# Two layers of an encoder trunk: one more pair of slabs by seven products, and single norms

## What is computed

```
h    = rmsnorm(x, gain)
proj = h @ w_in                     # 1024 -> 2304 columns in layer 0
q, k = rmsnorm per head of 64; v as it is
layer 0: heads 0-7 dilated windows with ALiBi; heads 8-15 banded GQA with a sink in the denominator
layer 1: dense GQA with rotary positions
x = x + concat(heads) @ w_out
x = x + sum over experts of weight * down(silu(gate(h2)) * up(h2))   # 32 experts, 2 of them for a token
```

## Time and profile before

| | |
|---|---|
| median of three executions | 618.3 us |
| the profiled execution, its own time | 618.75 us |
| span of its trace | 616.7 us |
| TensorE busy | 565.0 us (92%) |
| VectorE / ScalarE busy | 199.0 / 136.6 us |
| read from HBM | 231.6 MB |
| layer 0 mixer, layer 0 experts | 0 to 135 us, 135 to about 318 us |

### The profile page before, as it was taken

One profiled execution on the slowest core, in us unless ns is written; L12 is line 12 of the kernel. 1 busy time (PEld: TensorE's weight loads), 2 busy tenths in 40 slices (PEclk: granted clock), 3 DMA queues, 4 the chain that ended last, 5 costly groups with the idle time before them and its releaser, 6 DMA issues.

```text
span 616.7 us, 9572 instructions
## 1 busy us (share of the span) xinstructions
PE 565.0 (92%) x3884; PEld 373.5 (61%) x3884; DVE 199.0 (32%) x613; ACT 136.6 (22%) x353; POOL 9.9 (2%) x25
## 2 busy tenths in 40 slices
PE   8999999998999939998999999999899996997897
PEld 7887777783555333555468876779355435444454
DVE  3847555153111101111045687416212011011101
ACT  3144445341001101001031366524100110110101
POOL 1200000000000000000001000000000000000000
PEclk9999999999999969999999999999999997999899
DMA  8999786589999999999999994539999999999996
GB/s 316 424 421 420 282 361 218 204 329 409 430 430 425 442 425 424 433 435 409 421 415 421 421 421 206 207 122 354 373 427 431 428 435 424 430 426 432 413 421 271
DMA packets 24245, 233.39 MB, mean 378 GB/s; under 512 B 2688, under 2 KB 3328, under 8 KB 6656
## 3 DMA queue, kind: packets, MB, share of 16 engines
q1 hardware_dynamic: 22176, 227.14, 88.6%
q10 hardware_dynamic: 2016, 5.52, 2.5%
HBM read 231.60 MB, written 1.05 MB: 377 GB/s over the span
## 4 chain that ended last, share of the span: by engine, by line
PE 70%; DMA 20%; issue 4%; DVE 3%; ACT 3%; ACTq 0%; DVEq 0%
DMA ring<-in_moe_w 18%; PE banks L1118 13%; PE banks L851 10%; PE banks L984 8%; PE banks L1092 7%; PE banks L1188 6%; PE banks L1204 6%; PE banks L866 3%; PE banks L944 2%; PE banks L823 2%; PE banks L961 2%; PE banks L972 2%; DMA desk<-in_bias 1%; PE banks L1103 1%; PE banks L995 1%
## 5 line engine op out<-in xcount | busy, mean ns | idle before, releaser
L1118 PE MATMUL banks<-ring,desk 128*32 128x512 f32 x768 | 90.1, 608 | 5.4 <-DMA ring<-in_moe_w 5.3
L1448 ACT ACTIVATE desk<-banks 128x256 f32<-128x256 f32 x16 | 6.1, 383 | 272.7 <-PE banks L1118 272.7
L851 PE MATMUL banks<-ring,hT 128*128 128x256 f32 x288 | 65.3, 381 | 0.0
L1092 PE MATMUL banks<-desk,hT 128*128 128x128 f32 x384 | 49.5, 291 | 15.4 <-issue 15.4
L984 PE MATMUL banks<-heads,ring 128*128 128x256 f32 x256 | 61.9, 387 | 0.1
L1092 PEld LDWEIGHTS banks<-desk,hT 128*128 128x128 f32 x384 | 49.0, 208 | 16.7 <-issue 16.2
L851 PEld LDWEIGHTS banks<-ring,hT 128*128 128x128 f32 x288 | 53.7, 190 | 8.6 <-issue 1.8
L1118 PEld LDWEIGHTS banks<-ring,desk 128*32 128x32 f32 x768 | 23.7, 112 | 57.0 <-issue 51.9
L984 PEld LDWEIGHTS banks<-heads,ring 128*128 128x128 f32 x256 | 46.4, 190 | 12.6 <-issue 6.9
L1204 PE MATMUL banks<-desk 128*128 128x256 f32 x224 | 52.1, 386 | 0.0
L1204 PEld LDWEIGHTS banks<-desk 128*128 128x128 f32 x224 | 41.4, 190 | 16.8 <-issue 11.7
(11 more groups left out here) (201 smaller groups left out, 649.1 us busy)
## 6 DMA issues: line engine op xcount, KB each, us to landing
ring<-in_moe_w SPq DMA_DIRECT2D x66, 1024.0 KB, 26.7
ring<-in_moe_w SPq DMA_DIRECT2D x16, 4096.0 KB, 27.5
ring<-in_moe_w SPq DMA_DIRECT2D x17, 2048.0 KB, 12.7
ring<-in_ab_w_in SPq DMA_DIRECT2D x8, 1024.0 KB, 16.8
shared<-in_moe_w SPq DMA_DIRECT2D x8, 1024.0 KB, 7.6
shared<-in_moe_w SPq DMA_DIRECT2D x2, 4096.0 KB, 27.5
shared<-in_moe_w SPq DMA_DIRECT2D x3, 2048.0 KB, 11.3
ring<-in_c_w_in SPq DMA_DIRECT2D x5, 1024.0 KB, 20.3
```

Source lines behind the costliest of these rows:

```text
L851: ins = pe.matmul(bank2(SLAB_BANK[layer][s], NT)[:, t, :], hT[:, c, t * P:(t + 1) * P], w[:, c, :], start=(c == 0 and t == 0), stop=(c == ...
L1092: ins = pe.matmul(bank(2 + half)[:, c * P:(c + 1) * P], tokens[:, t, half * HALF + c * P:half * HALF + (c + 1) * P], onehot_of(rd, to)[:, ...
L1118: ins = pe.matmul(bank(0)[j * SLOTS:(j + 1) * SLOTS, :], gathered_of(rd, place)[:, c, j * SLOTS:(j + 1) * SLOTS], w[:, j, :], start=(c == ...
```

## The change

Slabs 5 and 6, and 7 and 8, become pairs, so that three pairs stand for two and no plain slab is left after slab 2. The differences of the weights get two buffers in turn (one more slot of the ring, SUMS_AT 15), and their four instructions are items of their own. Slab 5 (values) leaves its pair by a copy that scales. Slabs 6, 7 and 8 are normed one by one. ORDER_0 is written anew behind the first pair; layer 1 and the experts keep their code.

```diff
-PAIRED = ((3, 4), (6, 7))
-SUMS_AT = 16
+PAIRED = ((3, 4), (5, 6), (7, 8))
+SUMS_AT = 15
...
-        NORM = [[(0, 1), (3, 4), (6, 7), (8,)], ...
+        NORM = [[(0, 1), (3, 4), (6,), (7,), (8,)], ...
...
-            + each("norm", 0) + each("weights", 0) + parts(2, 0, 1, 2, 3)
+            + each("norm", 0) + sums(0, 3, 1, 2, 4) + parts(2, 0, 1, 2, 3)
             + each("turn", 0) + products(0, 1) + each("turn", 1) + products(0, 5)
-            + each("scores", 0) + products(0, 6, 7) + each("normalise", 0) + products(0, 2, 3)
-            + each("turn_prob", 0) + each("scores", 1) + products(0, 4) + parts(5, 0)
-            + each("prob_values", 0) + each("normalise", 1) + parts(5, 1) + each("norm", 1) + each("weights", 1) + parts(5, 2)
-            + each("turn_prob", 1) + parts(5, 3) + each("turn", 3) + products(1, 1) + each("turn", 4) + products(1, 5)
-            + each("scores", 2) + each("prob_values", 1) + products(1, 6, 7) + each("normalise", 2) + products(1, 2)
-            + each("turn_prob", 2) + each("scores", 3) + products(1, 3) + each("prob_values", 2)
-            + products(1, 4) + each("normalise", 3) + parts(8, 0) + each("residual", 0) + each("norm", 2)
-            + each("turn_prob", 3) + parts(8, 1, 2) + each("prob_values", 3) + parts(8, 3) + each("norm", 3)
-            + each("turn", 6) + rows((0, 0), (0, 1)) + each("turn", 7) + each("residual", 1) + rows((0, 2))
-            + each("scores", 4) + rows((0, 3), (1, 0), (1, 1)) + each("normalise", 4) + each("turn", 8) + rows((1, 2))
-            + each("turn_prob", 4) + each("residual", 2) + each("scores", 5) + rows((1, 3))
-            + each("prob_values", 4) + each("normalise", 5) + rows((2, 0), (2, 1))
-            + each("turn_prob", 5) + each("scores", 6) + rows((0, 4), (1, 4))
-            + each("prob_values", 5) + each("normalise", 6) + rows((2, 2), (2, 3))
-            + each("turn_prob", 6) + each("scores", 7) + rows((2, 4), (0, 5), (1, 5)) + each("prob_values", 6)
-            + each("normalise", 7) + rows((2, 5), (0, 6), (1, 6), (2, 6)))
+            + each("scores", 0) + products(0, 6, 7) + each("normalise", 0) + sums(1, 3, 1, 2) + products(0, 2, 3)
+            + each("turn_prob", 0) + each("scores", 1) + products(0, 4) + products(1, 1)
+            + each("prob_values", 0) + each("normalise", 1) + products(1, 5) + each("norm", 1) + products(1, 6)
+            + sums(1, 4) + each("turn_prob", 1) + products(1, 7) + sums(2, 3, 1, 2) + each("turn", 3) + products(1, 2)
+            + each("turn", 4) + each("prob_values", 1) + products(1, 3) + each("scores", 2) + products(1, 4)
+            + products(2, 1) + each("normalise", 2) + products(2, 5) + each("turn_prob", 2) + each("norm", 2)
+            + each("scores", 3) + products(2, 6) + each("prob_values", 2) + products(2, 7) + sums(2, 4)
+            + each("normalise", 3) + each("turn", 6) + products(2, 2) + each("residual", 0) + each("turn_prob", 3)
+            + products(2, 3) + each("prob_values", 3) + products(2, 4) + each("residual", 1) + each("norm", 3, 4)
+            + rows((0, 0), (0, 1), (0, 2), (0, 3), (1, 0)) + each("turn", 7) + rows((1, 1), (1, 2))
+            + each("turn", 8) + each("residual", 2) + each("scores", 4) + rows((1, 3), (2, 0), (2, 1), (2, 2))
+            + each("normalise", 4) + each("turn_prob", 4) + each("scores", 5) + rows((2, 3))
+            + each("prob_values", 4) + each("normalise", 5) + rows((0, 4), (1, 4))
+            + each("turn_prob", 5) + each("scores", 6) + rows((2, 4))
+            + each("prob_values", 5) + each("normalise", 6) + rows((0, 5), (1, 5))
+            + each("turn_prob", 6) + each("scores", 7) + rows((2, 5)) + each("prob_values", 6)
+            + each("normalise", 7) + rows((0, 6), (1, 6), (2, 6)))
...
         # product j == 5 of a pair after the first (PE)
-                    slab_taken(pe, 0, first - 1 if pair else 1)
+                    pe.wait_ge(s_tiles, 3 * pair)
...
         # ACT, product 2 and product 4 of a pair whose slab is "values"
+                        A.activation(values[0][:, 0, col:col + 4 * HD], x[:, 0, :], ACT.Copy, scale=rstd[:, 0:1])
+                            A.activation(values[0][:, 1, col:col + 4 * HD], widened, ACT.Copy, scale=rstd[:, 1:2])
...
         # ACT, residual
+                if layer == 0 and cp == 0:
+                    act.wait_ge(s_c11, len(PAIRED))
+                elif layer == 0 and cp == 1:
+                    act.wait_ge(s_tiles, 3 * len(PAIRED))
...
         # DVE, second tile of the pair's second slab: the wait inside buffer_turned now holds for "heads" and "keys"
-                if SLAB_PLAN[0][s][0] != "shared2":
+                if SLAB_PLAN[0][s][0] in ("heads", "keys"):
                     dve.wait_ge(s_hT_ps, turns_before(*NORMED[norm_slabs_before(0, s) - 1]))
```

More of the change, by code:

```diff
@@ L281, in hybrid_moe_kernel @@
         token_sum = sums_of[:, 0:UNIT].rearrange("p (i c t) -> p i c t", i=4, c=NC // 2)
-        weight_sum = sums_of[:, UNIT:UNIT + 3 * D].rearrange("p (i c n) -> p i c n", i=3, c=NC // 2)
+        weight_sums = sums_of[:, UNIT:UNIT + 6 * D].rearrange("p (r i c n) -> p r i c n", r=2, i=3, c=NC // 2)
         late_tiles = shared[:, 7168:7168 + 512].rearrange("p (t n) -> p t n", t=NT)
-        kept, widened = late_tiles[:, 0, :], late_tiles[:, 1, :]
-        fifth = shared[:, 7680:7680 + 256]
+        kept, widened = shared[:, 7680:7936], shared[:, 7936:8192]
+        fifth = shared[:, 3840:4096]
         LATER = (4, PAIRS)
@@ L556, in hybrid_moe_kernel @@
         SLAB_BANK = [[6, 7, 2, 6, 7, 6, 7, 6, 7], [2, 3, 6, 7, 6, 7]]
-        NORM = [[(0, 1), (3, 4), (6, 7), (8,)], [(0,), (2,), (3,), (4,), (5,)]]
+        NORM = [[(0, 1), (3, 4), (6,), (7,), (8,)], [(0,), (2,), (3,), (4,), (5,)]]
         def parts(slab, *which):
@@ L564, in products, with sums @@
             return [("product", pair, j) for j in which]
+        def sums(pair, *which):
+            return [("weights", pair, i) for i in which]
         def rows(*pieces):
@@ L657, in unnormed, with tile_of @@
             return buffers[:, norm_slabs_before(layer, s) % 2, :].rearrange("p (t n) -> p t n", t=NT)
+        def tile_of(s, t):
+            if SLAB_PLAN[0][s][0] == "values":
+                return widened
+            return late_tiles[:, t, :] if SLAB_PLAN[0][s][0] == "shared2" else unnormed(0, s)[:, t, :]
         def pair_banks(pair):
@@ L839, in slab @@
                     b = SLAB_BANK[layer][s]
[L840 to L843, removed]
+                    if b in SLAB_BANK[layer][:s]:
                         slab_taken(pe, layer, max(k for k in range(s) if SLAB_BANK[layer][k] == b))
@@ L860, in product @@
                 wa, wb = slab_weights(0, first), slab_weights(0, second)
+                t2, t3, t4 = [weight_sums[:, pair % 2, i, :, :] for i in range(3)]
                 low_half, high_half = slice(0, NC // 2), slice(NC // 2, NC)
@@ L871, in product @@
                     if pair:
-                        slab_taken(pe, 0, PAIRED[pair - 1][1])
+                        pe.wait_ge(s_c11, pair)
                     else:
@@ L877, in product @@
                 elif j == 5:
-                    slab_taken(pe, 0, first - 1 if pair else 1)
+                    if pair:
+                        pe.wait_ge(s_tiles, 3 * pair)
+                    else:
+                        slab_taken(pe, 0, 1)
                     pe.wait_ge(s_tsum, 1)
@@ L885, in product @@
                     pe.wait_ge(s_wsum, 4 * pair + 3)
-                    multiply(x[:, 1, :], token_sum[:, 1, :, :], weight_sum[:, 0, :, :]).then_inc(s_prod, 1)
+                    multiply(x[:, 1, :], token_sum[:, 1, :, :], t2).then_inc(s_prod, 1)
                 elif j == 7:
@@ L889, in product @@
                     pe.wait_ge(s_tsum, 3)
-                    multiply(y[:, 1, :], token_sum[:, 2, :, :], weight_sum[:, 1, :, :]).then_inc(s_prod, 1)
+                    multiply(y[:, 1, :], token_sum[:, 2, :, :], t3).then_inc(s_prod, 1)
                 elif j == 2:
@@ L900, in product @@
                     pe.wait_ge(s_wsum, 4 * pair + 4)
-                    multiply(y[:, 1, :], hT[:, high_half, rows_1], weight_sum[:, 2, :, :]).then_inc(s_used, 2)
+                    multiply(y[:, 1, :], hT[:, high_half, rows_1], t4).then_inc(s_used, 2)
             def turn(layer, s, half):
@@ L1303, in take_product @@
                     product_done(act, pair, 2)
-                    room_for(first)
-                    A.activation(unnormed(0, first)[:, 0, :], x[:, 0, :], ACT.Copy).then_inc(s_c11, 1)
+                    kind, _, col, _ = SLAB_PLAN[0][first]
+                    if kind == "values":
+                        A.activation(values[0][:, 0, col:col + 4 * HD], x[:, 0, :], ACT.Copy, scale=rstd[:, 0:1])\
+                            .then_inc(s_c11, 1)
+                        return
+                    if kind != "shared2":
+                        room_for(first)
```

(32 more changed lines are left out.)

2 lines of the change are left out of this document (removed).

## The result

The changed kernel takes 631.7 us (median of six executions, 630.84 to 634.34) against 618.41 for the kernel before (618.0 to 619.19): 2.24% slower, ratio 1.0224, 95% interval 1.0201 to 1.0248. The forecast was 625.8 with a range up to 631.0. The direction was right, the size was not: +13.3 us instead of +7.5. The profiled execution took 631.42 us, against 618.75 before.

A forecast was written before the change was run, and what follows sets the result against it. TensorE was taken to bound layer 0's mixer, each delay shifting everything behind it. Terms summed to +8.1 us, laid out in order +7.5; span 616.7 became 624.2, forecast 625.8 us, range 621.5 to 631.

The forecast's parts named there:

- 8 records fewer: TensorE, mixer of layer 0: 168 matmul records instead of 176, at 0.2175 us each, -1.74 us.
- `turn_prob` 3: TensorE waits there while DVE makes pair three's fourth weight difference before normalising heads 6 and 7: +1.05 us, bounds 0 to 1.25.
- `turn` 7 and 8: TensorE waits before each for the single norms of slabs 7 and 8: +0.65 us each, bounds 0.3 to 1 each.
- `turn_prob` 4: Its second head comes 4.7 us after its minima begin, with 4.1 us of work ahead: +0.65 us, 0.3 to 0.8.
- three waits for the attended pair: Rows behind `prob_values` 4, 5, 6 wait for ACT's copy, queued behind exponentials: 3 x 1.95 = +5.85 us.
- bias for `scores` 5: Bias load issued into the queue of six weight loads freed together, landing at 99.4: +1.7 us, 0 to 4.6.
- old waits: TensorE waits of the kernel before that go away, one of them 0.35 us before `turn_prob` 5: -0.73 us in all.
- The shift of everything behind: Weight stream restarts from used expert units, so a later mixer end moves that restart and all behind it equally: +7.5 us.
- Rival A: Not slower: weight transfers run on during the longer mixer and take up the delay, 618.3 or 616.6 us; chance 0.08.
- rival C: Stalls up to 3.6 us close together lower TensorE's granted clock, 5.2 us of full-speed work lost: 631 us; chance 0.11.
- rival D: More waits than found in DVE's queue of the second and third pair, up to 5 us again: 630 us; chance 0.11.
- Rival B: Not slower: new waits hidden if the attended pair's copy came right after `prob_values`, about 616.7 to 619 us; chance 0.07.

The follow-up runs named there:

- e7: Kernel before, with only the pieces of `rows` put where the change puts them, all slabs as before: 622.76 us, ratio 1.006.
- e1: Changed kernel with six pieces of `rows` moved so that none comes right behind the `prob_values` it needs: 626.82 us, ratio 1.0113.
- e2: Changed kernel with four weight loads (units 26 to 29) held until bias loads have landed: 627.81 us, ratio 1.0158.
- e3: Changed kernel with 18, 7 and 7 matmuls that nobody reads put into the three waits ahead of rows (0, 4), (0, 5), (0, 6): 629.29 us, ratio 1.016.
- e4: Changed kernel with DVE's fourth weight difference of the third pair moved behind `normalise` 3: 631.01 us, ratio 1.0195.
- e6: Changed kernel with the edits of e5 and e4, `scores` 4 right behind `turn` 7, and `turn` 8 later: 624.01 us, ratio 1.007.
- e5: Changed kernel with the edits of e1 and e2 together: 624.5 us, ratio 1.0087.

## Why the prediction was right in direction and wrong in size

The terms in us on TensorE, as predicted and as the traces have them, up to `turn_prob` 7:

| term | predicted | measured |
|---|---|---|
| 8 records fewer | -1.74 | -1.29 |
| `turn_prob` 3 | +1.05 | +0.77 |
| `turn` 7 and 8 | +1.3 | +1.59 |
| `turn_prob` 4 | +0.65 | +0.52 |
| three waits for the attended pair | +5.85 | +5.79 |
| bias for `scores` 5 | +1.7 | +2.93 |
| clock | 0 | +3.4 |
| old waits | -0.73 | -0.72 |
| waits too short for the table | 0 | +0.07 |
| from slab 0 to `turn_prob` 7 | +8.1 | +13.07 |
| slab 0 started earlier | 0 | -0.60 |
| sum | +8.1 | +12.47 |

The first line is TensorE's busy time in the two windows above (103.98 - 101.86 = +2.12) without the 3.41 that the low clock added. The count of 8 records was right, but the gain was 0.45 smaller than eight times 0.2175: the prediction had noted that some changes of operand go with the removed parts, and no run separates them.

**The waits: right.** Each was where it was said to be and had the releaser that was said. e7 makes such waits, 4.07 of the 5.79 us, without the rest of the change, and e1 takes them away, for new ones at `turn_prob` 4 and 5.

**The shift of everything behind: right.** From the first group load to the end of the span the kernel before takes 472.7 us (616.7 - 144.03), the one after 472.9; over all eleven traces it is 472.6 to 473.8, while that load moves between 144.03 and 156.50. Rival A would have made this number shrink as the load moved back. It doesn't, so what is late there is late at the end.

**The bias: mechanism right, size off.** The median latency of the earlier trace rows gave 5.6 us, and the load took 6.9. Of the six weight loads issued from 80.61 to 83.22 four had landed when the bias was issued at 93.52, the last of them at 92.92; the other two landed at 95.41 and 99.68, and the bias 0.76 after them. The term of 2.93 lies within its bounds of 0 to 4.6. e2 shows that these two are the cause: 3.4 us when they are held back. By the Trainium skill (DMA: Bandwidth & Descriptors, section Queues, rings and completion order) each DMA engine turns between its queues packet by packet; the landing at 98.3 that the prediction estimated from this was further off than the one by the median, 99.4, 100.44 being measured.

**The clock: the step that failed.** The forecast held TensorE at the full clock through all stalls, a term of 0 in its sum; rival C, with 0.11, named the fall. It came twice, 3.41 us at half rate from 104.93 and again from 115.17, with TensorE busy, so that half of 6.82 us was lost. By the timeline, rows (0, 4) and the `turn_prob` behind it took 1.45 and 0.28 longer than at the full clock, rows (0, 5) and its `turn_prob` 0.84 and 0.88: +3.4. e3 confirms the size by filling the waits (from the start of rows (0, 4) to `turn_prob` 7 there are 24.52 us after, 129.06 - 104.54, and 21.16 in e3, 126.27 - 105.11: 3.4 less). The argument against C was that each new stall is shorter than the one of 6.01 in the earlier trace rows; the one of 4.86 was enough. The trace of before could have warned of this: its clock fell at 221.53, when the wait of 6.01 had lasted 4.15 us. So rival C's mechanism was right. Its price of 5.2 us was too high, because it counted the whole fall as work lost, while TensorE was busy for only 4.45 us of it, of which the low clock took half:

```profile
221.50:231.80 10.30, 4.45 (x20) 4.40 (x21) 0.51 (x1) 0.00 (x0) 0.00 (x0) 0.50 0.99 425
```

With the clock's 3.4 and the 1.2 by which the bias was too small, the forecast of +7.5 becomes +12.1. That it comes near the measured +12.47 is partly luck, since the early start of slab 0 took 0.60 off; against the +13.07 of the stretch itself 1.0 is missing.

**Also claimed:** the old second pair's DVE work would cover the new; it did, no wait for a weight difference appears before `turn_prob` 3, so rival D fell. Rival B fell with the three waits. TensorE's busy time up to `turn_prob` 7 didn't shrink by 1.7 but grew by 2.1, since the low clock put more back.

**Open.** Which waits let the clock fall isn't settled. It fell within 0.4 us of the end of the wait of 4.86, in e4 inside a wait of 4.69, in e1 after waits of 1.69, 0.53 and 2.79, in e2 after three of 1.93 and in e6 after 0.63, 0.78 and 1.86. It did not fall in e7 (1.93, 1.07, 1.07) nor in e5 (1.68 and 0.52, later 1.55), nor in after itself behind the third wait, of 1.93. So the length of the last wait doesn't decide it. Nor is it settled how often it falls: only one execution of each kernel was profiled, and the mean granted clock of the six of after was 0.970 to 0.976, with the two of 634.3 us at 0.970 but one of 631.66 too, while the four of e3 had 0.978 to 0.981.

## What to carry to other kernels

A change that saves 8 matmuls (1.74 us) on the engine that bounds a stretch also moves when the results behind it come free; look at what stands next in that engine's list and put behind each producer only work that doesn't need it yet. Price every stall on TensorE twice, for its length and for the granted clock after it: here falls came behind one wait of 4.86 us, but also behind three of 1.93. A fall cost about half of the time that TensorE was busy in it. Before summing terms between two traces, look where the unchanged beginning stands in each. Before freeing many buffers at once, ask which small load will be issued into the transfers that this starts.

## What the hardware showed that was not expected

A 0.5 MB bias load on ACT's queue took 6.9 us while the last two of six 1 MB loads of SP's queue were in flight, and 3.4 us with these two held back (e2). TensorE's granted clock was at half (1.2 GHz) for 3.41 us after a wait of 4.86 us, again after one of 1.93 (e2: after three of 1.93), and for 6.83 us in e1 and e4. Matmuls whose results nobody reads, placed in those waits, kept it at 2.4 GHz and made the kernel 2.4 us faster (e3).
